# Weighted sums of gathered expert rows: from full 128x128 matmuls to 64x64 quarters of the array, two slots at a time

## What is computed

```
eidx = take_along_axis(cidx, sel)          # 8 heads x 16 experts of each token
g = softmax(top_s)
u = pu[eidx]; vv = pv[eidx]                # rows of 1024 floats each
a = gelu(einsum('thkd,td->thk', u, x))
return einsum('thk,thkd->td', g * a, vv)
```

## Time and profile before

| what | value |
|---|---|
| median of 3 runs | 1445.14 us (1444.89 to 1448.29) |
| profiled execution, span from first to last instruction | 1450.5 us, mean granted TensorE clock 0.903 |
| TensorE matmul busy | 1173.4 us, 81% |
| TensorE weight load busy | 590.3 us, 41% |
| VectorE busy | 893.8 us, 62% |
| GpSimd busy | 698.4 us, 48% |
| ScalarE busy | 141.9 us, 10% |
| HBM read | 446.62 MB, of which the gathers 402.68 MB |
| first gather issued, last one issued | 360.8 us, 1428.7 us |

### The profile page before, as it was taken

The page is one execution under the profiler, slowest core; times in us unless marked ns, Lnnn a source line. Parts: engine busy times, 40 slices in busy tenths (PEclk is TensorE's granted clock), DMA queues, the critical chain, the costliest instruction groups (busy, mean ns, idle before and its releaser), DMA issues.

```text
span 1450.5 us, 11611 instructions
## 1 busy us (share of the span) xinstructions
PE 1173.4 (81%) x3320; PEld 590.3 (41%) x3320; DVE 893.8 (62%) x2323; ACT 141.9 (10%) x304; POOL 698.4 (48%) x898
## 2 busy tenths in 40 slices
PE   7999999999999967777766867777777778777777
PEld 4545655677555533233322322332332233233332
DVE  4007446748468878788788795555555555555555
ACT  2101201311000100001010000000001000000000
POOL 0001120000556655665646746667674666576663
PEclk9999999899999998898888979889987888889889
DMA  8322446250989898998979989999997999999996
GB/s 315 116 84 85 60 150 259 87 232 2 372 349 377 343 392 324 395 394 330 402 307 391 386 346 386 383 392 391 397 397 306 399 401 379 391 399 381 392 387 265
DMA packets 68822, 454.84 MB, mean 314 GB/s; under 512 B 7240, under 2 KB 14764, under 8 KB 17328
## 3 DMA queue, kind: packets, MB, share of 16 engines
q0 software_dynamic: 55296, 402.68, 70.2%
q1 hardware_dynamic: 12656, 48.60, 9.8%
q10 hardware_dynamic: 832, 3.08, 0.6%
HBM read 446.62 MB, written 7.71 MB: 313 GB/s over the span
## 4 chain that ended last, share of the span: by engine, by line
PE 32%; DMA 28%; DVE 13%; POOL 13%; issue 10%; ACT 1%; POOLq 1%; DVEq 0%; SPq 0%
DMA arena<-in_peer_uv,arena 27%; PE ps L1064 11%; POOL arena L575 8%; PE ps L798 7%; PE ps L804 4%; POOL arena L574 4%; DVE arena L1500 4%; PE ps L918 2%; DVE arena L1508 2%; PE ps L1038 1%; POOL arena L563 1%; PE ps L1056 1%; DMA arena<-in_w_out 1%; PE ps L1011 1%; ACT arena L727 1%
## 5 line engine op out<-in xcount | busy, mean ns | idle before, releaser
L1064 PE MATMUL ps<-arena 128*128 128x512 f32 x1536 | 773.9, 663 | 248.7 <-DVE arena L1508 246.6
L1500 DVE CUSTOM_DVE_ANT_0 arena<-arena 128x1024 f32<-128x1024 f32 x376 | 455.9, 1227 | 298.2 <-DMA arena<-in_peer_uv,arena 297.4
L1064 PEld LDWEIGHTS ps<-arena 128*128 128x128 f32 x1536 | 319.1, 213 | 698.3 <-issue 403.7
L575 POOL DMA_INDIRECT arena<-in_peer_uv,arena x384 | 452.7, 1179 | 66.8 <-issue 32.8
L574 POOL TENSOR_TENSOR arena<-arena 128x1 f32<-128x1 f32 x384 | 153.4, 399 | 161.0 <-PE ps L1064 144.6
L563 POOL COPY arena<-arena 128x4 uint32 (+1 forms) x96 | 64.0, 666 | 172.0 <-DVE arena L1508 171.8
L798 PE MATMUL ps<-arena 128*128 128x384 f32 (+1 forms) x336 | 112.1, 492 | 0.0
L727 ACT ACTIVATE arena<-arena 128x4 f32<-128x4 f32 x94 | 19.3, 205 | 866.7 <-DVE arena L1500 866.7
L1508 DVE TENSOR_SCALAR arena<-arena 128x128 f32<-128x128 f32 x376 | 82.7, 293 | 3.3
L798 PEld LDWEIGHTS ps<-arena 128*128 128x128 f32 (+1 forms) x336 | 63.5, 192 | 43.9 <-issue 2.1
L585 POOL MEMSET arena<- 128x1 f32 x1 | 0.1, 98 | 140.7 <-DVE arena L1484 140.7
(11 more groups left out here) (235 smaller groups left out, 754.6 us busy)
## 6 DMA issues: line engine op xcount, KB each, us to landing
arena<-in_w_in SPq DMA_DIRECT2D x8, 2048.0 KB, 7.7
arena<-in_w_pq SPq DMA_DIRECT2D x4, 2048.0 KB, 9.9
arena<-in_peer_uv,arena POOLq DMA_INDIRECT x384, 10.0
arena<-in_w_out SPq DMA_DIRECT2D x3, 1024.0 KB, 7.4
arena<-in_state_C ACTq DMA_DIRECT2D x1, 2064.0 KB, 9.9
out_new_C_s<-arena SPq DMA_DIRECT2D x1, 2064.0 KB, 6.6
arena<-in_cache_k SPq DMA_DIRECT2D x4, 512.0 KB, 7.0
arena<-in_cache_v SPq DMA_DIRECT2D x1, 2048.0 KB, 16.7
```

What stands on the lines that cost most here:

```text
L575: nc.gpsimd.indirect_dma_start(slots[HALF * g + s], None, d["peer_uv"], bass.IndirectOffsetOnAxis(ap=isl[g][:, s:s + 1], axis=0)).then_inc ...
L1064: last = mm(ps[:, BANKS + half, :], diag[:, s, :], slots[s][:, DM + 512 * half:DM + 512 * half + 512], start=first and s == 0, stop=final ...
L1500: last = v.tensor_tensor_reduce(slots[s][:, 0:DM], slots[s][:, 0:DM], hn[:, t, :], 1.0, 0.0, ALU.mult, ALU.add, aslot[:, s:s + 1])
```

## The change

- `weigh` takes two slots at a time. A diagonal matrix has nothing off its diagonal, so tokens 0 to 63 need only the upper left quarter of it and tokens 64 to 127 the lower right one. Each slot and each half of the columns becomes two matmuls of 64 partitions by 64 columns of weights, with 512 moving columns. The first slot of a pair takes the two quarters of the array on its diagonal (c = r), the second the other two (c = 1 - r). The second slot's sums therefore land in the other tokens' PSUM partitions.
- The sums stand in four PSUM banks: one for each half of the 1024 columns and each half r of the tokens. In each bank one half of the partitions holds the sums of the even slots in their place and the other half those of the odd slots, crossed.
- The diagonals are 64 wide: `ident64` holds the identity of 64 in both halves of the partitions, copied from `ident` once.
- `finish` adds the four straight quarters from PSUM (four adds of 64 partitions), ScalarE moves the four crossed ones into an SBUF tile `cross` (which lies over `qqT`), and VectorE adds that with one addition of 1024 columns. TensorE's next tile waits for both.
- From `qq0` on the other PSUM tiles rotate over four banks (`LATE_BANKS`), and TensorE waits before the first sum until the last tiles in banks 4 and 5 are read.
- TensorE waits for the two diagonals of a pair at once and raises a new semaphore, `pair_seen`, at each pair.

```diff
-BANKS = 6
+BANKS, LATE_BANKS = 6, 4
+ACC = 4
+HP = 64
...
+    narrow = index["qq0"]
+    bank_of, held_by, holder = {}, {}, {}
+    for i, (n, _) in enumerate(plan):
+        k = i % BANKS if i < narrow else (i - narrow) % LATE_BANKS
+        bank_of[n], held_by[n] = k, holder.get(k)
+        holder[k] = n
+    final_wide = {k: [n for n, _ in plan[:narrow] if bank_of[n] == k][-1] for k in range(LATE_BANKS, BANKS)}
...
-        diag = at(o + 2608, SLOTS, P)
-        o += 2608 + SLOTS * P
+        diag = at(o + 2608, SLOTS, HP)
+        ident64 = at(o + 2608 + SLOTS * HP, HP)
+        cross = qqT.rearrange("p c t -> p (c t)")[:, 0:DM]
+        o += 2608 + SLOTS * HP + HP
...
+                act.wait_ge(used, HK * (n + 1))
+                for half in range(2):
+                    for r in range(2):
+                        tok, src = slice(HP * r, HP * r + HP), slice(HP - HP * r, 2 * HP - HP * r)
+                        act.activation(cross[tok, 512 * half:512 * half + 512], ps[src, ACC + 2 * half + r, :],
+                                       ACT.Copy).then_inc(cross_ok, 1)
                 act.wait_ge(ss1, 4 + HM + n)
...
             def weigh(n, i, first, final):
-                for s in range(SLOTS):
-                    pe.wait_ge(diag_ok, (n * ROUNDS + i) * SLOTS + s + 1)
+                done = (n * ROUNDS + i) * SLOTS
+                for a in range(0, SLOTS, 2):
+                    pe.wait_ge(diag_ok, done + a + 2)
+                    pe.sem_inc(pair_seen, 1)
                     for half in range(2):
-                        last = mm(ps[:, BANKS + half, :], diag[:, s, :], slots[s][:, DM + 512 * half:DM + 512 * half + 512],
-                                  start=first and s == 0, stop=final and s == SLOTS - 1, skip_group_check=True)
-                    last.then_inc(used, 1)
+                        cols_v = slice(DM + 512 * half, DM + 512 * half + 512)
+                        for s in (a, a + 1):
+                            for r in range(2):
+                                c = r if s == a else 1 - r
+                                tok = slice(HP * r, HP * r + HP)
+                                last = mm(ps[HP * c:HP * c + HP, ACC + 2 * half + r, :], diag[tok, s, :],
+                                          slots[s][tok, cols_v], start=first and a == 0, stop=final and a == SLOTS - 2,
+                                          skip_group_check=True)
+                            if half:
+                                last.then_inc(used, 1)
...
+                if i == 0:
+                    for k in range(LATE_BANKS, BANKS):
+                        was_read(pe, final_wide[k])
                 weigh(0, i, i == 0, i == ROUNDS - 1)
             assert order[0] == len(plan)
             for n in range(1, NT):
                 pe.wait_ge(acc_read, n)
+                pe.wait_ge(cross_ok, 4 * n)
...
-                        v.tensor_scalar(diag[:, s, :], ident, wslot_e[:, s:s + 1], None, ALU.mult).then_inc(diag_ok, 1)
+                        v.tensor_scalar(diag[:, s, :], ident64, wslot_e[:, s:s + 1], None, ALU.mult).then_inc(diag_ok, 1)
...
                 dve.wait_ge(used, HK * (n + 1))
-                v.tensor_tensor(xr[:, t, 0:512], xr[:, t, 0:512], ps[:, BANKS, :], ALU.add)
-                link(v.tensor_tensor(xr[:, t, 512:1024], xr[:, t, 512:1024], ps[:, BANKS + 1, :], ALU.add))
+                for half in range(2):
+                    for r in range(2):
+                        tok, c = slice(HP * r, HP * r + HP), slice(512 * half, 512 * half + 512)
+                        last = v.tensor_tensor(xr[tok, t, c], xr[tok, t, c], ps[tok, ACC + 2 * half + r, :], ALU.add)
+                link(last)
                 v.engine_nop().then_inc(acc_read, 1)
+                dve.wait_ge(cross_ok, 4 * (n + 1))
+                link(v.tensor_tensor(xr[:, t, :], xr[:, t, :], cross, ALU.add))
...
+            for r in range(2):
+                v.tensor_copy(ident64[HP * r:HP * r + HP, :],
+                              ident[HP * r:HP * r + HP, HP * r:HP * r + HP]).then_inc(ident64_ok, 1)
+            dve.wait_ge(ident64_ok, 2)
             add_mix("y", *tt[2])
```

More of the change, by code:

```diff
@@ L391, in encoder_kernel @@
         acc_read = sem("tile_sum_read")
+        cross_ok = sem("crossed_sums_moved")
+        pair_seen = sem("pairs_begun")
+        ident64_ok = sem("half_identity_ready")
         y_ok = sem("y_ready")
@@ L407, in bank @@
         def bank(name):
-            return ps[:, index[name] % BANKS, :]
+            return ps[:, bank_of[name], :]
         chunk_slot = {c: c % 3 for c in range(9)} | {11: 2, 12: 1, 13: 3, 14: 4}
@@ L765, in begin @@
                 order[0] += 1
-                if index[name] >= BANKS:
-                    was_read(pe, plan[index[name] - BANKS][0])
+                if held_by[name]:
+                    was_read(pe, held_by[name])
                 return bank(name)
```

## The result

The changed kernel is slower. Its median is 1468.07 us (1466.02 to 1471.1), the kernel before beside it 1446.72 us; the ratio is 1.0138, with a 95% interval of 1.0086 to 1.0190. Run twice more beside other kernels it gave 1.0104 (1.0073 to 1.0136) and 1.0102 (1.0060 to 1.0145). So it costs 14 to 21 us against the kernel before that ran beside it, where 8.5 us less was forecast.

What follows compares the result with a forecast made beforehand. It took the DMA gathers (98% busy) as the bound, with TensorE's time to the first freed slot in the loop. Terms -9 - 3 - 2 + 5.5 = -8.5 us from 1445.1 gave 1436.6, predicted as 1437; range 1406 to 1460.

Steps and rivals of the forecast that it cites:

- Steady rounds: Some 30 rounds without a routing step: 21.25 us each instead of 21.56, -9 us, bounds -47 and +55.
- rival 3: Second group's first slot freed 1.8 us later at the low clock: rounds 22.0, in all +14, 1459 us; chance 0.17.
- Diagonals: VectorE's building of diagonals, now 64 wide: cheaper around routing steps, -2 us (0 to -5); TensorE's start unchanged.
- Packing: Weighted sums on TensorE: four quarter matmuls run at once, a pair taking 1.7 us at high clock, 3.4 at low.
- rival 4: Quarter matmuls' weight loads not hidden: 0.9 to 1.5 us before the first free slot, about 1480 us; chance 0.04.
- Rivals 4 and 5: The second of these: quarters don't run four at a time, near 1730 us one by one, 1530 in twos; chance 0.08.
- First slot of a group: Freeing of slots: slot 0 no sooner, slots 2 and 3 1 to 3 us sooner at the low level.
- First rounds: About three rounds where query matmuls wait behind the sums: sums ending 3.5 us sooner give -3 us.
- End of a tile: Finishes and last groups: +2.5 us per finish, +7.5 for three, -3 middle tile, +1 last round; sum +5.5.
- The rest: PSUM bank rotation, old-bank waits, small identity, pair semaphore, instruction count: 0, at most +2 us.
- Rival 1: Slots 1 to 3 issued close behind slot 0 keep the queue full: rounds 20.4, in all -34, 1411 us; chance 0.20.
- The clock: TensorE idles before both groups, so both start low; second group's first issue moves from 2.41 to about 4.2 us.

Runs made afterwards that it cites:

- experiment 2: Kernel before, slots 1 to 3 of each group summing only 344 of 1024 columns, so half the work without packing: ratio 1.0021.
- Experiment 5: Changed kernel with three extra matmuls, results unused, behind each group in the middle and last tile: ratio 1.0012.
- experiment 4: Changed kernel with six extra matmuls, results unused, behind each group in the middle and last tile: ratio 0.9747.
- Experiment 6: Changed kernel with TensorE waiting for one diagonal at a time instead of two: ratio 1.0065, then 1.0063; with six extra matmuls a group added, 0.9778.
- experiment 3: Kernel before with three extra matmuls, results unread, behind each group in the middle and last tile: ratio 0.9735.

## Why the prediction was wrong

**The failed step is "Steady rounds".** It took 21.25 us a round, -9 us in 30 rounds. Over 23 rounds the kernel before has 21.48 and the changed one 21.94, 21.96 and 21.85 in its three profiles: +0.37 to +0.48 a round, +8.5 to +11 us. So this step is off by 17 to 20 us, of the 23 to 30 by which the forecast of -8.5 missed the measured +14 to +21. (The 30 rounds were too many as well: the routing reaches into the fifth round of the middle tile, which leaves ten rounds there, fourteen in the last tile and one in the first.) Its first input came true: both groups start at the low level, and the second one's first issue comes 4.1 us after TensorE's start. What failed is what followed from that, and a wait that the prediction had put at nothing.

- *The reserve.* "It has room" (3.85 us) and "the thinner queue before the second group takes 0.2 of it back". The reserve was read off one round of the earlier trace rows. On average the gather of slot 4 took 8.44 us from its issue to its dot in the kernel before, and 6.14 at the least: 2.3 us of reserve. Counted from the group's fourth dot its issue came 0.8 to 1.0 us later, and 0.3 to 0.4 of that reached the next dot 4 (14.00 us from dot 7 to that dot, then 14.38, 14.39 and 14.30). The gap before dot 4 grew from 2.67 to 2.81, 3.24 and 2.92 us. It is 2.8 us or more in every kernel whose second group starts low and 2.7 or less where it starts high (table). With the packing left out, experiment 2 shows +0.21 us a round, at the edge of what one profile can tell. Experiment 5 takes the loss back out of the packed kernel. That is rival 3's mechanism (rounds at 22.0, +14, 1459), which had 0.17: it described the result best. Its +14 is the lower end of the measured difference, its 1459 lay 4 to 9 us below the changed kernel's medians.
- *The gain.* "The gap between dots 0 and 3 closes (-0.5)": it went from 7.95 to 7.84, 7.67 and 7.85 us. Slots 2 and 3 were to be issued 1 to 3 us sooner; counted from the fourth dot they came 0.4 and 0.5 us sooner (10.69 and 12.49 to 10.28 and 11.99). The packed group spends most of its time at the low level: 5.9 us on average, where a group wholly at the high one takes 3.66 (experiment 4). The full one reached the high level for its last slots (9.24 us in the earlier trace rows is 3.4 for one slot and some 1.9 for each of the others). In the second group, which had started high, slots 6 and 7 were not issued sooner but 1.0 and 1.1 us later (9.10 and 10.74 to 10.08 and 11.86). The prediction had no term for that.
- *TensorE's start.* "The first diagonal pair is ready about when one diagonal was: no change of TensorE's start" under Diagonals. TensorE starts 2.44 us after the fourth dot, not 2.17. The second diagonal, 0.25 us long, stands in the path of every group. Experiment 6 prices it: 0.1 to 0.2 us a round in its profiles (21.78 and 21.69 against 21.92 in the mean), 7 to 8 us in the total; the step had put it at nothing.

**Packing** was right. Four quarters run at once: at the low level slot 0 was free 3.76 us after TensorE's start in the round shown (1310.95 to 1314.71), the last pair took 1.95 us at the high one, and a whole group at the high one 3.66 us in experiment 4, where four full-width slots took 7.13. The loads of 64 columns take 0.22 us at the low level and lie under the matmuls. The Trainium skill, "TensorE: Matmul & The Clock Gate", Part 3, which lets a load run ahead only where row groups differ, would have made this rival 4 (1480); with two quarters in the same rows, 32 loads lie within the 6.38 us of the matmuls, so the trace disagrees here too. Rivals 4 and 5 are out.

**First slot of a group** was right: pairs free slot 0 no sooner. **First rounds** (-3) and **Diagonals** (-2) came in part: the first fifteen rounds took 345.7, 347.2 and 349.1 us in the three profiles of the changed kernel and 345.3 and 345.4 in the two packed ones with fillers, which are the same up to there. The kernel before took 349.2, and 349.4 in experiment 3, the same up to there too. That is -2.8 in the mean against -5, in values that scatter by 4 us; which of the two terms it belongs to was not tried. In the tile's total it is hidden by the last round with the finish in it, 33.1 to 33.3 us in those five profiles against 29.5 and 30.9 in those two. **End of a tile** was right in size: +2.8 us per finish against 2.5; that first finish +3.0; the middle tile's last group took 5.85 us instead of 9.69, and that round 33.2, 33.1 and 32.1 instead of 35.1; behind the last dot +2.9 (11.61 to 14.48), and +4.6 and +4.4 in the two later profiles of the changed kernel, whose last pair took 3.69 and 3.45 us at the low clock. Together that is +4.0 to +5.6 against +5.5. **The rest**: of the sums' 493.0 us of idle time 486.2 end with a diagonal, so a wait on a bank has at most 7 us of it.

**Rival 1** (0.20) had its high-clock sign named: "first issues at 2.5 us". They came, with 34 to 39 us less, only once TensorE had other work. **The clock**, the step that the whole result hangs on, was foreseen but priced one-sidedly: the earlier trace rows against the earlier trace rows show that the level is worth 1.7 us a slot, and the text called that "in the loop" for the first group and a reserve for the second. The Trainium skill says on the same page, Part 1, under HAM oscillation, that a loop whose bursts of matmuls are shorter than its waits for the DMA starts each burst at the low clock. The low starts are here, the condition is not. In the kernel before, the first groups ran 9.2 us after 4.3 us of idle time and 18 of 23 started low; in the changed one, first and second groups ran 5.9 us each after 6.0 and 4.5 us. The mean clock in the last tile was 0.87, then 0.71, and 1.00 with the fillers.

What stays open: how much of the loss is the level alone. Experiment 2 gives +2 us in the total (-2 to +8), experiment 5 gives back 13, and experiment 6 gives 7 to 8 to the wait for the pair, so the two causes overlap. Nor is it known how much a given depth of the queue hides, and why the gather of slot 0, issued only 0.2 to 0.3 us later after the fourth dot, reached its dot 0.5 to 0.7 us later (13.54 us from dot 3 to the next dot 0, then 14.10, 14.28 and 14.00).

## What to carry to other kernels

Where TensorE frees the buffers of a DMA loop, as here, its latency to the first release counts, not its busy time; work taken off it can lower its clock and lengthen that latency. Look at the granted clock and the idle time before each burst, and price a cut in work by the level at which the rest will then start. Before speeding such an engine up, try the opposite: a few matmuls whose result nobody reads gave 2.7 to 2.9% here, where the packed form with half the work lost 1.0 to 1.4%. And look at what a wait for two things adds when one was enough.

## What the hardware showed that was not expected

- DMA engines 98% busy at 390 GB/s were not at their limit: with earlier issues the same gathers ran at 418 to 421 GB/s, a round of 21.5 us became 20.0.
- The two levels switch within a round, and each group goes its own way: three filling matmuls in the packed kernel brought only the second groups back to the high level, six brought both; in the full-width kernel two a group brought both.
- The filling cost nothing in the first tile's rounds with routing either: the tile took 376.2 us with two matmuls a group and 376.5 with three, 378.7 and 380.2 without.
